# A hybrid decoder trunk on one core: the variance of five layer norms summed with the squares as stationary operand, and the output stored in four parts

## The chip, the cores and the metric

The kernel runs on one NeuronCore of a Trainium2 chip. The metric is the device time of one execution in microseconds (us). The engines are TensorE (PE, its weight loads PEld), VectorE (DVE), ScalarE (ACT), GpSimd (POOL) and SyncE (SP), which only issues DMAs here. Each engine works through its own queue in order; they meet at semaphores.

## The reference, cut to what matters

A two-layer trunk on 1024 tokens of 1024 features (f32). It has five layer norms: one on the input, and two in each layer.

```python
def layer_norm(x, g, b):
    mu = xf.mean(-1, keepdims=True)
    var = jnp.square(xf - mu).mean(-1, keepdims=True)
    return ((xf - mu) * lax.rsqrt(var + LN_EPS) * g + b)

x = layer_norm(x, ln_emb_g, ln_emb_b)
for i in range(2):
    mix = hybrid_mixer(x, ...)
    x = layer_norm(ALPHA * x + mix, ln1_g[i], ln1_b[i])
    ffn = square(relu(x @ mlp_w1[i])) @ mlp_w2[i]
    ple = sigmoid(x @ pe_gate[i] + pe_gate_b[i]) * (p[i] @ pe_proj[i])
    x = layer_norm(ALPHA * x + ffn + ple, ln2_g[i], ln2_b[i])
```

## The kernel before

Activations lie with features on partitions: `Y[:, kt, token]` is feature tile `kt` of 8 (`KT`), and the tokens are two halves of 512 (`hs(hf)`). A sum over features is therefore a product on TensorE: `mean_ones` (128x128, all 1/1024) is stationary, a 128x512 tile moves, and every partition of the PSUM bank receives the sum, already spread over partitions. An f32 product is two PE instructions in the trace.

`layer_norm(u)` is a function in each of four engines' programs; u counts the norms 0 to 4. They share two-buffered tiles `SQ` and run as follows:

- PE: the mean of each half (L621 for u=0, L624 else) into banks 4 and 5. Then, for each half and each `kt`, `mean_ones` times the squares (L629), accumulated in bank 6 + hf.
- DVE: 16 subtractions of the mean (L1613); then for each half, wait for the deviation `STD`, take its reciprocal over 128x512 (L1620), and multiply the eight tiles by it (L1624, or L1628). In norms 1 and 3 the multiplication (L1628), gain and offset (L1631) and the low part `XL` (L1636) of each tile are interleaved on DVE. `XL` of tile kt waits for its high part `XH`, which ACT copies (L1141).
- ACT: squares of half 0 (L1131), square root of each half's bank (L1134), then 16 writes: `XH` in norms 1 and 3, or gain and offset into `X` (L1144) in norms 0, 2 and 4. Norm 0 computes sine tables between root and writes (L1151).
- POOL: the squares of half 1 (L1433).

With the tile counter as semaphore value, square kt waits until the product of square kt - 2 is done.

What follows each norm: norm 0 and norm 2 are followed by the input projection (L669), which takes `X` tile by tile; norm 2 also by the jump back of the layer loop. Norms 1 and 3 are followed on PE by blocks (mt, hf) in the order (0,0), (1,0), (0,1), (1,1), (2,0) and so on: two products with `PE_IN` (L1107, into bank 4 + b; they wait for both square roots while mt < 2), and 24 products of `dense` (L1087 to L1089: high x high, high x low, low x high of each of 8 tiles, fp32r, which is one PE instruction each). Norm 4 is followed by one store of `X`, 4 MB, from SP's queue (L609).

Of the kernel before, what the change touches and what calls it, by code (L numbers as in the profile page):

```python
# [22 lines left out]
ALU = mybir.AluOpType  # L23
ACT = mybir.ActivationFunctionType
# [181 lines left out]
def trunk(nc, xT, pT, pos, w_in, w_uq, w_lr, w_pool, w_out, w_gate, w_pe, w_1, w_2, par, emb, con1, con2, out):  # L206
    cs_dram = nc.dram_tensor("cs_scratch", (2, P, S), F32, kind="Internal").ap()
    with ExitStack() as ctx:
# [3 lines left out]
        def sem(name):  # L212
            return ctx.enter_context(nc.semaphore(name))
# [148 lines left out]
        def met_value(L, n):  # L362
# [3 lines left out]

        ln_sq_later, ln_sum = sem("ln_sq_later"), sem("ln_sum")
        LN_SUMS = 2 + 2 * FB
        ln_mu, ln_xc, ln_sq, ln_sqf, ln_var, ln_std, ln_xn, ln_out = (
            sem(n) for n in ("ln_mu", "ln_xc", "ln_sq", "ln_sqf", "ln_var", "ln_std", "ln_xn", "ln_out"))  # L370

# [170 lines left out]
        @block.sync  # L542
        def _(e):
            e.dma_start(C1[:, :], con1).then_inc(con_landed, 16)
            e.dma_start(EMB[:, :], emb).then_inc(con_landed, 16)
            e.dma_start(BZ[:, 0, :].bitcast(I32), pos.broadcast_to([P, S])).then_inc(pos_landed, 16)
            for hf in range(2):
                e.dma_start(Y[:, :, hs(hf)], xT[:, :, hs(hf)]).then_inc(x_landed[hf], 16)

            def weight_block(L, i):  # L550

                e.wait_ge(w_used, L * W_LAYER + (i + 1))
                settle(e)
                if i < ZW:
                    src = w_in[ds(L, 1), IN_BLOCK[i]]
                elif i < ZW + N_WOUT:
                    src = w_out[ds(L, 1), i - ZW]
                else:
                    src = w_gate[ds(L, 1), i - ZW - N_WOUT]
                e.dma_start(WR[:, i % RING, :, :], src[0]).then_inc(w_landed[i % RING], 16)  # L560

            with e.Fori(0, DEPTH) as L:
                for i in range(RING):
                    weight_block(L, i)

                e.wait_ge(met, met_value(L, -1))
                e.wait_ge(cs_stored, 32)
                e.dma_start(CT[:, :], cs_dram[0]).then_inc(tables_landed, 16)
                e.dma_start(ST[:, :], cs_dram[1]).then_inc(tables_landed, 16)
                e.dma_start(UQ[:, 3:7, :, :], w_uq[ds(L, 1), :, 6:10][0]).then_inc(uqi_landed, 16)  # L570
                e.dma_start(UQ[:, 0:3, :, :], w_uq[ds(L, 1), :, 0:3][0]).then_inc(uq_landed, 16)
                e.dma_start(PAR[:, :], par[ds(L, 1)][0]).then_inc(par_landed, 16)

                for hf in range(2):
                    e.wait_ge(kik_done, L * 2 + (hf + 1))
                    e.dma_start(A3[HD:P, 2, hs(hf)], A3[0:HD, 2, hs(hf)]).then_inc(dup_landed, 16)
                    e.dma_start(IK2[0:HD, hs(hf)], IK2[HD:P, hs(hf)]).then_inc(dup_landed, 16)
                    if hf == 0:
                        weight_block(L, 4)
                        weight_block(L, 5)  # L580
                for i in range(6, ZW + RING - 1):
                    weight_block(L, i)
                e.wait_ge(turned.full, turned.written(L, LAST_Q))
                e.dma_start(LWA[:, :, :, :], w_lr[ds(L, 1)][0, :, 0:2]).then_inc(lora_landed, 16)
                e.dma_start(PW[:, :, :], w_pool[ds(L, 1)][0]).then_inc(lora_landed, 16)
                e.dma_start(LG[:, :, :], w_lr[ds(L, 1)][0, :, 2]).then_inc(lora_landed, 16)
                weight_block(L, ZW + RING - 1)
                e.wait_ge(met, met_value(L, 0))
                for c in range(2):
                    blocks = con2[chunk(c), 0:(6 + LEVELS) * P].rearrange("p (k w) -> p k w", w=P)  # L590
                    e.dma_start(C2P[chunk(c), 0:6 + LEVELS, :], blocks[:, :, chunk(c)]).then_inc(rwkv_landed, 16)
                e.dma_start(i64, con2[:, NC2 - CH:NC2]).then_inc(rwkv_landed, 16)
                e.wait_ge(met, met_value(L, 2))
                settle(e)
                for i in range(ZW + RING, MLP0 - GAP):
                    weight_block(L, i)
                    if i == ZW + N_WOUT + 1:
                        e.wait_ge(d_full[3], L * D_USES + N_WOUT // 2)
                        settle(e)
                        e.dma_start(PE_IN[:, :, :], pT[ds(L, 1)][0]).then_inc(pe_landed, 16)  # L600
                        e.dma_start(PEW[:, :, :, :], w_pe[ds(L, 1)][0]).then_inc(pe_landed, 16)
                with e.Fori(0, FB) as f:
                    for i in range(N_F):
                        e.wait_ge(w_used, L * W_LAYER + f * N_F + (MLP0 + i + 1))
                        src = w_1 if i < FT else w_2
                        e.dma_start(WR[:, i % RING, :, :], src[ds(L * FB + f, 1), i % FT][0])\
                         .then_inc(w_landed[i % RING], 16)
            e.wait_ge(ln_out, 16 * (1 + 2 * DEPTH))
            e.dma_start(out, X[:, :, :]).then_inc(out_stored, 16)  # L609
            e.wait_ge(out_stored, 16)  # L610


        @block.tensor
        def _(e):
            def layer_norm(u, landed=None, sums=None, total=None):

                for hf in range(2):
                    if landed:
                        e.wait_ge(landed[hf], 16)
                        for kt in range(KT):  # L620
                            mm = e.matmul(BK_[4 + hf], mean_ones, Y[:, kt, hs(hf)], start=kt == 0, stop=kt == KT - 1)  # L621
                    else:
                        e.wait_ge(ln_sum, sums + (hf + 1))
                        mm = e.matmul(BK_[4 + hf], mean_ones, total[:, hf, :], start=True, stop=True)  # L624
                    mm.then_inc(ln_mu, 1)
                for hf in range(2):
                    for kt in range(KT):
                        e.wait_ge((ln_sq, ln_sq_later)[hf], u * KT + (kt + 1))
                        e.matmul(BK_[6 + hf], mean_ones, SQ[:, 2 * hf + kt % 2, :], start=kt == 0, stop=kt == KT - 1)\  # L629
                         .then_inc(ln_sqf, 1)  # L630

            e.sem_inc(w_used, RING)
            for b in zbank + wide + [third, narrow, turned] + prep + rb:
# [347 lines left out]
            with e.Fori(0, DEPTH) as L:  # L981
# [119 lines left out]
                for mt, hf in [(0, 0), (1, 0), (0, 1), (1, 1)] + [(mt, hf) for mt in range(2, KT) for hf in range(2)]:  # L1101
                    b = 2 * (mt % 2) + hf
                    if mt < 2:
                        e.wait_ge(ln_std, (L * 2 + 2) * 2)
                    e.wait_ge(pe_free[b], L * 4 + (mt // 2 + 1))
                    for kt in range(2):
                        mm = e.matmul(BK_[4 + b], PEW[:, mt, kt, :], PE_IN[:, kt, hs(hf)], start=kt == 0, stop=kt == 1)  # L1107
# [16 lines left out]
        def _(e):  # L1124
            def layer_norm(u, gain=None, offset=None, dst=None, high=None, between=None):

                for kt in range(KT):
# [1 line left out]
                    if kt >= 2:  # L1129
                        e.wait_ge(ln_sqf, u * 16 + (kt - 1))  # L1130
                    e.activation(SQ[:, kt % 2, :], Y[:, kt, hs(0)], ACT.Square).then_inc(ln_sq, 1)  # L1131
                for hf in range(2):
                    e.wait_ge(ln_sqf, u * 16 + KT * (hf + 1))
                    e.activation(STD[:, hf, :], BK_[6 + hf], ACT.Sqrt, bias=LN_EPS).then_inc(ln_std, 1)  # L1134
                if between:
                    between()
                for n in range(2 * KT):
                    hf, kt = n // KT, n % KT
                    if high is not None:
                        e.wait_ge(ln_out, u * 16 + (n + 1))  # L1140
                        e.activation(high[:, kt, hs(hf)], Y[:, kt, hs(hf)], ACT.Copy).then_inc(high_x, 1)  # L1141
                    else:
                        e.wait_ge(ln_xn, u * 16 + (n + 1))
                        e.activation(dst[:, kt, hs(hf)], Y[:, kt, hs(hf)], ACT.Identity, bias=offset(kt),  # L1144
                                     scale=gain(kt)).then_inc(ln_out, 1)

            def tables():

# [274 lines left out]
        def _(e):  # L1423
            def layer_norm(u):

                for kt in range(KT):
                    e.wait_ge(ln_xc, u * 16 + (KT + kt + 1))
                    if kt >= 2:
                        e.wait_ge(ln_sqf, u * 16 + (KT + kt - 1))
# [176 lines left out]
        def _(e):  # L1606
            def layer_norm(u, between=None, affine=None, high_before=0):
# [6 lines left out]
                         .then_inc(ln_xc, 1)  # L1614
                if between:
                    between()
                for hf in range(2):
                    q = hs(hf)
                    e.wait_ge(ln_std, u * 2 + (hf + 1))
                    e.reciprocal(RST[:, hf, :], STD[:, hf, :])  # L1620
                    e.drain()
                    if not affine:
                        for kt in range(KT):
                            e.tensor_tensor(Y[:, kt, q], Y[:, kt, q], RST[:, hf, :], ALU.mult).then_inc(ln_xn, 1)  # L1624
                    else:
                        for n in range(KT + 3):
                            if n < KT:
                                e.tensor_tensor(Y[:, n, q], Y[:, n, q], RST[:, hf, :], ALU.mult).then_inc(ln_xn, 1)  # L1628
                            if 1 <= n <= KT:
                                gain, offset = affine(n - 1)  # L1630
                                e.tensor_scalar(Y[:, n - 1, q], Y[:, n - 1, q], gain, offset, ALU.mult, ALU.add)\  # L1631
# [504 lines left out]
```

## Time and profile before

| | us |
|---|---|
| median of 3 runs | 3576.71 |
| lowest and highest | 3575.73, 3585.78 |
| the profiled execution | 3576.34 |
| its span | 3574.3 |
| mean granted TensorE clock | 0.965 of full |

A profile is one execution. The chart of waits and the chain of work name, for each idle time, the instruction whose semaphore ended it. The granted clock of a stretch is 1.00 when TensorE is given 2.4 GHz and 0.50 at 1.2 GHz; a value between is a mean over the stretch.

### The profile page before, as it was taken

The numbers are of one execution on the slowest core, as the hardware profiler recorded it, in microseconds if no ns is written. First come the engines' busy times: TensorE is split into PE (matmuls) and PEld (weight loads), VectorE is DVE, ScalarE is ACT, GpSimd is POOL, SyncE is SP. The second block draws the span as 40 slices with busy tenths as digits, with TensorE's granted clock in tenths as the row PEclk, the third lists the DMA queues.
The fourth block names the chain that finished last, engine by engine and source line by source line (L and its number), as shares of the span: only waits on it lengthen the run. The fifth ranks groups of instructions, "written<-read, shape, count | busy, mean of one in ns | idle before, by whom it ended". The sixth has DMA issues, their size and how long they took to land.

```text
span 3574.3 us, 61403 instructions
## 1 busy us (share of the span) xinstructions
PE 3274.0 (92%) x23080; PEld 2373.5 (66%) x23080; DVE 1913.2 (54%) x3061; ACT 1053.9 (29%) x1857; POOL 1146.4 (32%) x952
## 2 busy tenths in 40 slices
PE   7989967999999999999989998689899999999997
PEld 3444435876577888888735444368675788888884
DVE  5788996444623333333467899854526133333335
ACT  3333334442212211211235343344402111221212
POOL 1175632641212222222114755155222122222221
PEclk9999979999999999999999899799999999999998
DMA  3110000001111111111111001000011111111111
GB/s 123 45 33 21 29 23 6 0 1 36 48 36 48 47 47 47 53 47 48 40 55 33 28 24 33 11 6 0 7 31 58 42 51 49 47 47 47 48 46 47
DMA packets 43861, 132.72 MB, mean 37 GB/s; under 512 B 9280, under 2 KB 11840, under 8 KB 43072
## 3 DMA queue, kind: packets, MB, share of 16 engines
q1 hardware_dynamic: 37280, 122.41, 10.5%
q10 hardware_dynamic: 6432, 8.40, 0.9%
q8 instruction: 84, 1.38, 0.2%
q14 instruction: 65, 0.53, 0.0%
HBM read 117.15 MB, written 5.24 MB: 34 GB/s over the span
## 4 chain that ended last, share of the span: by engine, by line
PE 59%; DVE 14%; issue 10%; DVEq 10%; POOLq 2%; ACT 1%; POOL 1%; DMA 1%; PEldq 0%; ACTq 0%; SPq 0%; PEld 0%
DVE M L1715 8%; DVEq L1719 8%; PE wide L1087 7%; PE bank L1089 7%; PE bank L1087 7%; PE bank L1088 7%; PE wide L1089 7%; PE wide L1088 7%; PE wide L799 3%; DVE PB L1735 2%; PE wide L629 2%; PE bank L799 2%; POOLq L1591 1%; DVE WK L1717 1%; DVEq L1716 1%
## 5 line engine op out<-in xcount | busy, mean ns | idle before, releaser
L1590 POOL TENSOR_TENSOR WL<-WR,WH 128x1024 fp32r<-128x1024 f32 x160 | 403.1, 2519 | 1479.2 <-ACT WH L1385 1478.5
L669 PE MATMUL wide<-X,WR 128*128 128x512 f32 (+1 forms) x1088 | 504.7, 608 | 11.6 <-ACT X L1144 9.4
L1385 ACT ACTIVATE WH<-WR 128x1024 fp32r<-128x1024 f32 x160 | 168.2, 1053 | 735.6 <-PE bank L1089 430.2
L2019 DVE TENSOR_TENSOR RB<-RB 128x512 f32<-128x512 f32 x128 | 88.5, 692 | 549.0 <-ACT RB L1411 549.0
L669 PEld LDWEIGHTS wide<-X,WR 128*128 128x128 f32 x1088 | 202.7, 196 | 246.9 <-issue 220.9
L1715 DVE MAX8 M<-WK 128x8 f32<-128x512 f32 (+5 forms) x342 | 314.9, 921 | 23.7
L1717 DVE MATCH_REPLACE8 WK<-M,WK 128x512 f32<-128x512 f32 (+5 forms) x342 | 309.5, 905 | 1.2 <-issue 1.2
L1087 PE MATMUL wide<-XH,WH 128*128 128x512 f32 x640 | 261.6, 409 | 18.1 <-POOLq L1591 9.5
L1087 PE MATMUL bank<-XH,WH 128*128 128x512 f32 x640 | 255.7, 400 | 0.0
L1089 PE MATMUL wide<-XH,WL 128*128 128x512 f32 x640 | 252.8, 395 | 0.0
L1088 PE MATMUL wide<-XL,WH 128*128 128x512 f32 x640 | 252.5, 395 | 0.0
L1089 PE MATMUL bank<-XH,WL 128*128 128x512 f32 x640 | 249.2, 389 | 0.0
L1088 PE MATMUL bank<-XL,WH 128*128 128x512 f32 x640 | 249.0, 389 | 0.0
L1087 PE MATMUL wide<-HH,WH 128*128 128x512 f32 x512 | 201.3, 393 | 0.0
L1088 PE MATMUL wide<-HL,WH 128*128 128x512 f32 x512 | 199.4, 389 | 0.0
L1089 PE MATMUL wide<-HH,WL 128*128 128x512 f32 x512 | 199.4, 389 | 0.0
L1089 PE MATMUL bank<-HH,WL 128*128 128x512 f32 x512 | 199.2, 389 | 0.0
L1088 PE MATMUL bank<-HL,WH 128*128 128x512 f32 x512 | 199.2, 389 | 0.0
L1087 PE MATMUL bank<-HH,WH 128*128 128x512 f32 x512 | 199.2, 389 | 0.0
L2032 DVE TENSOR_TENSOR Y<-Y,bank 128x512 f32<-128x512 f32 x128 | 87.9, 687 | 171.1 <-PE bank L1089 171.1
L799 PE MATMUL wide<-SH 64*64 64x64 f32 x3840 | 153.2, 220 | 21.2 <-POOL SH L1525 14.6
L2032 DVE TENSOR_TENSOR Y<-Y,wide 128x512 f32<-128x512 f32 x128 | 88.0, 687 | 153.7 <-PE wide L1089 153.7
(318 smaller groups left out, 6399.2 us busy)
## 6 DMA issues: line engine op xcount, KB each, us to landing
WR<-in_w SPq DMA_DIRECT2D x128, 512.0 KB, 3.5
WR<-in_w_in SPq DMA_DIRECT2D x34, 512.0 KB, 3.5
WR<-in_w_out SPq DMA_DIRECT2D x16, 512.0 KB, 3.5
WR<-in_w_gate SPq DMA_DIRECT2D x16, 512.0 KB, 5.5
Y<-in_xT SPq DMA_DIRECT2D x2, 2048.0 KB, 13.3
out_T<-X SPq DMA_DIRECT2D x1, 4096.0 KB, 11.1
QZS<-QZ ACTq DMA_DIRECT2D x48, 64.0 KB, 2.0
QZS<-QZ ACTq DMA_DIRECT2D x64, 48.0 KB, 1.9
```

Of the source, the lines that this page charges most:

```text
L669: mm = e.matmul(BK_[hf][:, 0:q.stop - q.start], WR[:, i % RING, kt, :], X[:, kt, q], start=kt == 0, stop=kt == KT - 1)
L799: mm = e.matmul(BK_[bank][chunk(c), j * CH:(j + 1) * CH], lhs[chunk(c), 2 * j + g, :], rhs[chunk(c), 2 * j + g, :], start=True, stop=True)
L1087: e.matmul(BK_[b], WH[:, s, w, :], high[:, kt, q], start=kt == 0, stop=False)
L1088: e.matmul(BK_[b], WH[:, s, w, :], low[:, kt, q], start=False, stop=False)
L1089: mm = e.matmul(BK_[b], WL[:, s, w, :], high[:, kt, q], start=False, stop=kt == kts - 1)
L1385: e.activation(WH[:, split_seq(i) % 2, :, :], WR[:, i % RING, :, :], ACT.Copy).then_inc(w_high, 1)
L1590: e.tensor_tensor(WL[:, s, :, :], WR[:, i % RING, :, :], WH[:, s, :, :].bitcast(F32), ALU.subtract)
L1715: e.max(M8[:, :], src)
L1717: e.match_replace(work, M8[:, :], src, DROPPED if drop else BIG)
L1719: e.drain()
L2019: e.tensor_tensor(RB[:, b, :], RB[:, b, :], RB[:, b, :], ALU.mult).then_inc(square_ready, 1)
L2032: e.tensor_tensor(Y[:, i, hs(hf)], Y[:, i, hs(hf)], BK_[b], ALU.add).then_inc(d_free[b], 1)
```

## The change

Squares and sums: the squares become the stationary operand, 128 tokens at a time, and two columns of `mean_ones` move. So for each half and `kt` there are four products of 128x2, and the bank holds, for token tile t, its sum in column 2t (tokens on partitions). Square root and reciprocal are then taken of 128x8 rather than 128x512. `spread_inverse` brings the inverse back to all partitions: four products of 128x128 with the inverse, broadcast, as stationary and the identity as moving operand, into the same bank. DVE multiplies by that bank.

Order: PE runs `spread_inverse` of half 0 behind tile 1 of half 1, and that of half 1 behind its last tile. ACT takes the squares of the odd tiles of half 1, POOL keeps the even ones. DVE takes the inverse of half 1 behind the multiplication of tile 5 of half 0. In norms 2 and 4, ACT writes three tiles of `X` before the square root of half 1. The store waits for a quarter of `X` four times and stores each by itself.

```diff
+            for n in range(KT // 2, 2 * KT + 1, KT // 2):
+                k, q = slice(...), hs((n - 1) // KT)
+                e.wait_ge(ln_out, 16 * 2 * DEPTH + n)
+                e.dma_start(out[:, k, q], X[:, k, q]).then_inc(out_stored, 16)
# tensor
-                        e.matmul(BK_[6 + hf], mean_ones, SQ[:, 2 * hf + kt % 2, :], start=kt == 0, stop=kt == KT - 1)
+                        for t in range(LN_TOK):
+                            mm = e.matmul(BK_[6 + hf][:, 2 * t:2 * t + 2], SQ[:, 2 * hf + kt % 2, t * P:(t + 1) * P],
+                                          mean_ones[:, 0:2], ...)
+                        mm.then_inc(ln_sqf, 1)
+                        if (hf, kt) in ((1, 1), (1, KT - 1)):
+                            spread_inverse(u, int(kt > 1))
+            def spread_inverse(u, hf):
+                e.wait_ge(ln_inv, u * 2 + (hf + 1))
+                for t in range(LN_TOK):
+                    mm = e.matmul(BK_[6 + hf][:, t * P:(t + 1) * P],
+                                  STD[:, hf, 2 * t:2 * t + 1].broadcast_to([P, P]), ident, start=True, stop=True)
+                mm.then_inc(ln_spread, 1)
# the two PE_IN products of mt < 2
-                        e.wait_ge(ln_std, (L * 2 + 2) * 2)
+                        e.wait_ge(ln_xn, (L * 2 + 1) * 16 + (KT * (hf + 1) if mt else 1))
# scalar, after the squares of half 0
+                ahead = 3 if high is None and not between else 0
+                later_square(1)
+                deviation(0)
+                for kt in range(3, KT, 2):
+                    later_square(kt)
+                for n in range(ahead):
+                    write_out(n)
+                deviation(1)
+                if between:
+                    between()
+                for n in range(ahead, 2 * KT):
+                    write_out(n)
# gpsimd
-                for kt in range(KT):
+                for kt in range(0, KT, 2):
# vector
+                def invert(hf):
+                    e.wait_ge(ln_std, u * 2 + (hf + 1))
+                    e.reciprocal(STD[:, hf, 0:2 * LN_TOK], STD[:, hf, 0:2 * LN_TOK]).then_inc(ln_inv, 1)
+                invert(0)
                 for hf in range(2):
-                    e.wait_ge(ln_std, u * 2 + (hf + 1))
-                    e.reciprocal(RST[:, hf, :], STD[:, hf, :])
+                    e.wait_ge(ln_spread, u * 2 + (hf + 1))
-                            e.tensor_tensor(Y[:, kt, q], Y[:, kt, q], RST[:, hf, :], ALU.mult).then_inc(ln_xn, 1)
+                            e.tensor_tensor(Y[:, kt, q], Y[:, kt, q], BK_[6 + hf], ALU.mult).then_inc(ln_xn, 1)
+                            if (hf, kt) == (0, KT - 3):
+                                invert(1)
```

## Rows read from the trace of the kernel before

**Rows 1.** Lines view: instructions, shapes, count; busy us and mean ns; idle before and its releaser.

```profile
L629 PE MATMUL wide<-SQ,C 128*128 128x512 f32 x160 | 81.2, 634 | 9.1 <-POOL SQ L1433 8.4
L1433 POOL TENSOR_TENSOR SQ<-Y 128x512 f32<-128x512 f32 x40 | 47.9, 1221 | 104.6 <-DVE Y L1613 86.6 <-PE wide L629 16.6 <-issue 1.4
L1620 DVE RECIPROCAL RST<-STD 128x512 f32<-128x512 f32 x10 | 33.5, 3348 | 1.0 <-ACT STD L1134 0.4 <-issue 0.2
L1131 ACT ACTIVATE SQ<-Y 128x512 f32<-128x512 f32 x40 | 25.1, 630 | 85.0 <-DVE Y L1613 70.1 <-PE wide L629 14.9
```

**Rows 2.** A stretch of norm 1: length, busy of PE, PEld, DVE, ACT, POOL; clock; DMA.

```profile
964.00:979.00 15.00, 13.55 (x51) 8.90 (x49) 14.00 (x24) 6.53 (x10) 0.00 (x0) 1.00 0.00 1
```

**Rows 3.** Timeline of norm 1: start, length, engine, line, tiles, count, idle and releaser.

```profile
930.73 9.42 PE L629 MATMUL wide<-SQ,C 128*128 128x512 f32 x20
...
942.53 2.36 DVE L1628 TENSOR_TENSOR Y<-Y,RST 128x512 f32<-128x512 f32 x2
...
948.18 0.60 ACT L1134 ACTIVATE STD<-wide 128x512 f32<-128x512 f32 x1 [9.11 <-PE wide L629]
...
979.93 1.88 PE L1107 MATMUL wide<-PE_IN,PEW 128*128 128x512 f32 x4
...
987.13 1.45 PE L1107 MATMUL wide<-PE_IN,PEW 128*128 128x512 f32 x3
```

**Rows 4.** Timeline of PE around products of two columns and of 128.

```profile
63.28 3.73 PE L656 MATMUL wide<-X,WR 128*128 128x128 f32 x32
...
73.38 3.78 PE L679 MATMUL bank<-A,UQ 128*128 128x128 f32 x16 [4.51 <-DMA UQ<-in_w_uq]
...
483.67 2.84 PE L969 MATMUL wide<-C,SH 128*128 128x2 f32 x24
...
802.25 6.72 PE L969 MATMUL wide<-C,SH 128*128 128x2 f32 x48
```

**Rows 5.** Stretches within those of 802 us, columns as Rows 2.

```profile
805.00:806.00 1.00, 1.00 (x11) 1.00 (x11) 1.00 (x1) 0.19 (x1) 0.01 (x1) 1.00 0.00 0
807.00:808.00 1.00, 1.00 (x7) 1.00 (x6) 1.00 (x2) 0.00 (x0) 0.00 (x0) 0.50 0.00 0
812.00:813.00 1.00, 1.00 (x2) 0.34 (x1) 0.38 (x1) 0.00 (x0) 0.00 (x0) 0.53 0.00 0
```

**Rows 6.** Line view of L969 from 2557.1 to 2559.4: min/median/max ns, first and last start.

```profile
L969 PE MATMUL wide<-C,SH x13: 251/353/353, 2556.9 to 2559.3; 128*128 128x2 f32 x13
```

**Rows 7.** Line view of a small reciprocal.

```profile
L1982 DVE RECIPROCAL G<-G x2: 441/442/443, 815.2 to 2566.0; 128x48 f32<-128x48 f32 x2
```

**Rows 8.** Timeline of norm 0 and what follows it.

```profile
44.08 3.35 DVE L1620 RECIPROCAL RST<-STD 128x512 f32<-128x512 f32 x1 [0.16 <-issue]
...
49.43 1.28 ACT L1151 ACT_TABLE_LOAD   x1
...
53.23 11.39 ACT L1144 ACTIVATE X<-Y,EMB 128x512 f32<-128x512 f32 x16 [0.41 <-ACT BZ L1151]
```

**Rows 9.** Timeline behind norm 2, where the layer loop jumps back.

```profile
1803.98 9.92 PE L669 MATMUL wide<-X,WR 128*128 128x512 f32 x16 [4.07 <-ACT X L1144]
...
1816.30 1.28 ACT L1257 ACT_TABLE_LOAD   x1 [4.48 <-issue]
1817.60 0.60 ACT L1257 ACTIVATE PB<-wide 128x512 f32<-128x512 f32 x1
```

**Rows 10.** Line view: the loop's branch on PE's queue.

```profile
L981 PEldq COMPARE_BRANCH  x2: 67/1760/3454, 1800.2 to 3551.2; - x2
```

**Rows 11.** Timeline of norm 4 and the store.

```profile
3533.23 9.42 PE L629 MATMUL wide<-SQ,C 128*128 128x512 f32 x20
...
3551.44 11.38 ACT L1144 ACTIVATE X<-Y,PAR 128x512 f32<-128x512 f32 x16
```

**Rows 12.** The page's DMA issues: tiles, count, KB each, us to landing.

```profile
WR<-in_w SPq DMA_DIRECT2D x128, 512.0 KB, 3.5
out_T<-X SPq DMA_DIRECT2D x1, 4096.0 KB, 11.1
```

More of the change, by code:

```diff
@@ L368, in trunk @@
         LN_SUMS = 2 + 2 * FB
+        ln_inv, ln_spread = sem("ln_inv"), sem("ln_spread")
+        LN_TOK = HALF // P
+        SQ_ACT = [kt % 2 for kt in range(KT)]
         ln_mu, ln_xc, ln_sq, ln_sqf, ln_var, ln_std, ln_xn, ln_out = (
@@ L607, in _ @@
                          .then_inc(w_landed[i % RING], 16)
-            e.wait_ge(ln_out, 16 * (1 + 2 * DEPTH))
-            e.dma_start(out, X[:, :, :]).then_inc(out_stored, 16)
-            e.wait_ge(out_stored, 16)
+            for n in range(KT // 2, 2 * KT + 1, KT // 2):
+                k, q = slice((n - 1) % KT // (KT // 2) * (KT // 2), (n - 1) % KT + 1), hs((n - 1) // KT)
+                e.wait_ge(ln_out, 16 * 2 * DEPTH + n)
+                e.dma_start(out[:, k, q], X[:, k, q]).then_inc(out_stored, 16)
+            e.wait_ge(out_stored, 4 * 16)
         @block.tensor
@@ L627, in layer_norm @@
                     for kt in range(KT):
-                        e.wait_ge((ln_sq, ln_sq_later)[hf], u * KT + (kt + 1))
-                        e.matmul(BK_[6 + hf], mean_ones, SQ[:, 2 * hf + kt % 2, :], start=kt == 0, stop=kt == KT - 1)\
-                         .then_inc(ln_sqf, 1)
+                        if hf == 0:
+                            e.wait_ge(ln_sq, u * (KT + KT // 2) + (kt + 1))
+                        elif SQ_ACT[kt]:
+                            e.wait_ge(ln_sq, u * (KT + KT // 2) + (KT + kt // 2 + 1))
+                        else:
+                            e.wait_ge(ln_sq_later, u * (KT // 2) + (kt // 2 + 1))
+                        for t in range(LN_TOK):
+                            mm = e.matmul(BK_[6 + hf][:, 2 * t:2 * t + 2], SQ[:, 2 * hf + kt % 2, t * P:(t + 1) * P],
+                                          mean_ones[:, 0:2], start=kt + t == 0, stop=kt + t == KT + LN_TOK - 2)
+                        mm.then_inc(ln_sqf, 1)
[7 more added lines that the diff above has]
+                mm.then_inc(ln_spread, 1)
             e.sem_inc(w_used, RING)
@@ L1131, in layer_norm, with later_square, deviation, write_out @@
                     e.activation(SQ[:, kt % 2, :], Y[:, kt, hs(0)], ACT.Square).then_inc(ln_sq, 1)
-                for hf in range(2):
+                def later_square(kt):
+                    e.wait_ge(ln_xc, u * 16 + (KT + kt + 1))
+                    if kt >= 2:
+                        e.wait_ge(ln_sqf, u * 16 + (KT + kt - 1))
+                    e.activation(SQ[:, 2 + kt % 2, :], Y[:, kt, hs(1)], ACT.Square).then_inc(ln_sq, 1)
+                def deviation(hf):
                     e.wait_ge(ln_sqf, u * 16 + KT * (hf + 1))
[L1134 to L1137, printed above, removed]
+                    e.activation(STD[:, hf, 0:2 * LN_TOK], BK_[6 + hf][:, 0:2 * LN_TOK], ACT.Sqrt, bias=LN_EPS)\
+                     .then_inc(ln_std, 1)
+                def write_out(n):
                     hf, kt = n // KT, n % KT
@@ L1616, in layer_norm @@
                     between()
+                def invert(hf):
+                    e.wait_ge(ln_std, u * 2 + (hf + 1))
+                    e.reciprocal(STD[:, hf, 0:2 * LN_TOK], STD[:, hf, 0:2 * LN_TOK]).then_inc(ln_inv, 1)
+                invert(0)
                 for hf in range(2):
                     q = hs(hf)
-                    e.wait_ge(ln_std, u * 2 + (hf + 1))
-                    e.reciprocal(RST[:, hf, :], STD[:, hf, :])
-                    e.drain()
+                    e.wait_ge(ln_spread, u * 2 + (hf + 1))
                     if not affine:
                         for kt in range(KT):
-                            e.tensor_tensor(Y[:, kt, q], Y[:, kt, q], RST[:, hf, :], ALU.mult).then_inc(ln_xn, 1)
+                            e.tensor_tensor(Y[:, kt, q], Y[:, kt, q], BK_[6 + hf], ALU.mult).then_inc(ln_xn, 1)
+                            if (hf, kt) == (0, KT - 3):
+                                invert(1)
                     else:
@@ L1627, in layer_norm @@
                             if n < KT:
-                                e.tensor_tensor(Y[:, n, q], Y[:, n, q], RST[:, hf, :], ALU.mult).then_inc(ln_xn, 1)
+                                e.tensor_tensor(Y[:, n, q], Y[:, n, q], BK_[6 + hf], ALU.mult).then_inc(ln_xn, 1)
+                            if (hf, n) == (0, KT - 3):
+                                invert(1)
                             if 1 <= n <= KT:
```

## The prediction

> **What bounds the kernel now.** I read the lines view first. The variance products, L629, hold TensorE for 81 us over five norms; half 1's squares come from POOL at 1.04 us each and more, half 0's from ACT at 0.63, and the ten reciprocals of 128x512 cost 3.35 us each, 33.5 in all [rows 1]. The timeline then shows what a norm waits for. In norm 1 the sums start at 930.7, the first multiplication follows at 942.5, the root of half 1 comes at 948.2, 9.1 us after ACT fell idle, and the block (1,1), the first that no longer waits for the norm, starts at 979.9 [rows 3]. Half 1's sums wait for POOL's squares (8.4 of L629's 9.1 idle us) [rows 1]. Behind that DVE is busy for 14.0 of 15 us, for eight tiles of half 1, and sets the end; TensorE is at 2.4 GHz there [rows 2]. So a norm is paced by DVE, POOL and the round trips among them. The change attacks these, and pays on TensorE.
>
> **What a group of sums costs.** Before, one tile costs two instructions, in steady flow one per 0.43 us. Now it is a group of four products, eight instructions of 128x2. The key sums L969 have the same form, also with squares as stationary operand: 24 in 2.84 us, or 0.112 each after the last one's 0.25 [rows 4]. So a group is 0.90 us at full clock, as before. But TensorE doesn't stay at full clock in such products. In the run of 48 from 802.25, PE is busy without a gap, yet the granted clock is 1.00 at 805 and 0.50 at 807, that is 4 us after the first of them; it comes back at 812.9, after some 4 us of products of 512 columns, which start where the 48 end, at 808.9 [rows 4, 5]. The run of 24 ended before that. At 1.2 GHz twelve intervals take 2.4 us, 0.20 to 0.21 each [rows 6], and a group 1.7 us.
>
> Two rules of the Trainium skill bear here. The first is in "TensorE: Matmul & The Clock Gate", section "Back-to-back issue gap": a gap of about 60 cycles for 1 to 64 columns. By that a group would be 8 x 25 ns = 0.2 us; the trace has 0.90, and goes before it. The second is in the same page's "What's actually happening": the engine's clock is throttled by default, and its activity releases it. Taken at its word, an engine without a gap would keep its clock; rows 5 say otherwise. Both are rivals below.
>
> Each norm will have 64 such products in a row, with gaps. I let the clock fall 3 us into them, since they come in looser order than in the key sums. Bounds: at once, and 4 us. Each microsecond later saves 0.9.
>
> **What the rest costs.** `spread_inverse`, eight instructions with 128 columns: 32 of L656 took 3.73 us at full clock, 16 of L679 took 3.78 in a half-clock stretch [rows 4]; so 1.05 us or 1.9 with its tail. The reciprocal of 128x48 takes 0.44 and that of 128x512 3.35; on their line one of 128x8 takes 0.2 [rows 1, 7]. The root of 128x512 takes 0.60 [rows 3]; I give that of 128x8 0.2, the two with their signals 0.5. Below 0.1 or up to 0.8 for both changes a norm by 0.4. Where the changed code multiplies from a PSUM bank, I take no difference.
>
> **Norm 4 at half clock.** Sums start at 3533.2 [rows 11]. In 3 us 3.3 groups pass, 4.7 more take 8.0: half 0 is summed at 3544.4, 11.2 us after the start, where norm 1 before had its first multiplication behind a reciprocal of 3.35 at 11.8. The next two groups, already queued ahead of the spread, take 3.4, the spread 1.9: multiplications from about 3549.4. The remaining six groups take 10.2: half 1 summed at 3559.6. DVE has long done tile 5 and stands at the inverse of half 1; root and inverse 0.5, spread 1.9: 3562.1. ACT has written three tiles ahead and has 13 left from 3559.9 at 11.38/16 = 0.71 [rows 11]: last tile at 3569.3, against 3562.8 (3551.4 + 11.4) before, +6.5. POOL's halved work is not the bound any more.
>
> The store: 4 MB took 11.1 us, 512 KB take 3.5 [rows 12]. On that line 1 MB takes 4.6. The four parts become ready each 2.8 us and move 1 MB at some 2.6 us, so the last one doesn't queue: -6.5 us. Bounds: 3.5 for the quarter, and 11.1 were pieces of 2 KB that bad. Norm 4 in sum: 0, with bounds -1 and +6.
>
> **Norms 1 and 3.** The same to the end of half 1's sums: start 930.7, half 0 at 941.9, spread done 947.2 (before, multiplying began at 942.5), half 1 at 957.4 (before 948.2 [rows 3]). Here two queues hurt. On ACT, `XH` stands behind the root of half 1, as before, so DVE, which needs `XH` of tile 0 behind tile 3, stalls until about 958. And the inverse of half 1 stands on DVE behind tile 5, which is two tiles of 1.9 us (15 us for eight [rows 2]) after the stall: 961.5. PE waits for it, idle, before its second spread: 963.4. Only behind that come the blocks. Before, block (0,0) started at 950 and ran in step with DVE's tiles. Now two `PE_IN` products at half clock (3.4 us), 24 dense products, of which 4 are still slow (0.43) and 20 at 0.23: 973.1. (A block took 7.2 us, 1.7 of it for the four `PE_IN` instructions: 5.5/24 = 0.23 [rows 3].) I give the clock 5 us of this to come back (4 in rows 5). Blocks (1,0) and (0,1) cost 7.2 each; start of (1,1) at 987.5 against 979.9 [rows 3]: +7.6 for each of the two. DVE ends half 1's `XL` at 983 and is covered. Bounds: +5 with the clock falling at 4 us, +9.5 when it falls at once and comes back late.
>
> **Norm 0.** DVE computes the last angle before its inverse until 44.0 [rows 8], and PE waits for it before the first spread. Sums of half 0 and two groups are done by then, so: spread at 45.5 (DVE may be up to 1 us earlier, with fewer POOL squares beside it; I don't count it), six groups 10.2, root, sine tables 3.8 (49.4 to 53.2): first `X` at 60.5, where it was 54.0 (53.2 and its own 0.8) [rows 8]: +6.4. ACT's 16 writes and the projection shift with it. Bounds +5 and +7.5.
>
> **Norm 2.** As norm 4, its second spread ends near 1811.1. Then the loop's branch: it held PE's queue for 3.45 us and the first product came 4.0 after PE's last norm product [rows 9, 10]. So L669 starts at 1815.1, against 1804.0: +11.1. But it then finds `X` complete, and what follows was not PE alone: ACT, behind its last write at 1818.2, takes 4.5 + 1.3 for its own branch and table [rows 9], and copies the projection (`PB`) at about 1824.7, against 1817.6 [rows 9]. So +7.1; bounds +5 and +11.
>
> **Sum**, against the profiled execution: 6.4 + 7.6 + 7.1 + 7.6 + 0 = +28.7. The execution took 3576.3 us (span 3574.3 and 2.0 around it), and 3576.3 + 28.7 = 3605.0. It was within 0.4 us of the median of 3576.7, so I predict **3605**. Other stretches of half clock may move by a few us as everything behind shifts.
>
> **Rivals.**
>
> *The clock holds* (the end on the other side). One mechanism: TensorE stays at 2.4 GHz through the sums. For it: 24 products in 2.84 us; against: the run of 48 from 802 us [rows 4, 5] and a second one, at half clock by 2557 us [rows 6]. Behind it stands the second rule above, of the Trainium skill. Then a norm is faster: half 0's sum in 7.7, half 1 done 16.2 after the start, not 26.4. Norm 4: last write 3559.5, -3.3, and -6.5 of the store: -9.8. Norms 1 and 3: (1,1) at 974.0, -5.9 each. Norm 2: +0.3. Norm 0, tied to the angle: +1.6. Sum -19.7: 3557. It decides from where less than some 4 us of a norm's PE time is slow.
>
> *The clock falls, but late* or rises between the groups, about half of the loss: 3572 to 3588, even at a saving of half the slow groups.
>
> *Narrow products are cheap*, by the skill's gap rule. A group of 0.2 us would be paced by squares at 0.63 to 0.65, half clock or not: sixteen tiles in about 11 us rather than 16: another 4 us for each of norms 1 to 4, 3541. The trace's own 0.112 us per instruction speaks against it.
>
> *The store's small pieces*: a quarter as slow as the whole, +6.5: 3611; it adds to my case and lies in the range.
>
> **How the numbers follow.** My case 0.82, of it 3594 to 3614; the late fall 0.08; the clock holds 0.08; cheap products 0.02. The range is 3589 to 3614: it holds my case with its bounds and part of the late fall, near 0.8. A measurement here can tell 0.3%, 10.7 us. Slower by more: 0.82 and 0.01 of the late fall, 0.83. Within: 0.07. Faster: 0.10.
>
> **What would show it.** In the profile after: granted clock at 0.50 from some 3 us into each norm's products of two columns until about 5 us into the products behind it; mean clock below 0.965. Roots of half 1 near 26 us after the sums start, not 17. In norms 1 and 3 an idle PE of about 4 us before the second spread, ended by DVE's inverse, and DVE waiting for `XH`. L669 behind norm 2 starting 11 us late, `PB` 7. The store's last part landing in 4 to 5 us. I am wrong if the clock is 1.00 through a norm's sums; then all but norm 0 and 2 gain.

## The result, and the profile after

The changed kernel takes 3608.35 us (median, 3606.55 to 3612.89, 4 runs) against 3579.45 us beside it (3575.73 to 3585.78, 4 runs): a ratio of 1.0081, with an interval of 1.0062 to 1.0100. Predicted were 3605 us, between 3589 and 3614, with 0.83 for slower. The profiled execution has a span of 3604.6 us, 30.2 more than before, and a mean granted clock of 0.949 instead of 0.965.

The lines view of the kernel after, with the columns of [rows 1]:

```profile
L640 PE MATMUL wide<-C,SQ 128*128 128x2 f32 x640 | 126.2, 334 | 0.5
L650 PE MATMUL wide<-C,STD 128*128 128x128 f32 x80 | 20.7, 440 | 10.0 <-DVE STD L1661 10.0
L1475 POOL TENSOR_TENSOR SQ<-Y 128x512 f32<-128x512 f32 x20 | 21.1, 1053 | 163.4 <-DVE Y L1655 87.2 <-PE wide L640 76.1
L1685 DVE TENSOR_TENSOR XL<-Y,XH 128x512 fp32r<-128x512 f32 x32 | 22.0, 687 | 13.7 <-ACT XH L1170 13.4
```

L640 holds TensorE for 126.2 us, where L629 held it for 81.2 [rows 1], and hardly ever waits: of the 9.1 idle us before, 8.4 of them ended by POOL's squares, 0.5 are left. The waits went elsewhere. POOL now idles for 76.1 us until TensorE frees a square's buffer (16.6 before), so the producer that seemed to bound the sums waits for them. L650, the spread, waits 10.0 us for DVE's small reciprocal, and L1685 waits 13.4 us for `XH`.

The clock, norm 1 in stretches (columns of [rows 2]):

```profile
938.70:940.40 1.70, 1.64 (x14) 1.64 (x14) 1.70 (x4) 1.09 (x3) 0.97 (x1) 0.92 1.01 424
940.40:954.60 14.20, 14.20 (x68) 14.20 (x68) 6.82 (x13) 3.98 (x8) 2.08 (x2) 0.50 0.53 219
954.60:974.50 19.90, 15.66 (x68) 14.65 (x69) 10.79 (x20) 5.51 (x10) 2.23 (x2) 0.51 0.00 1
974.50:995.00 20.50, 20.50 (x83) 15.21 (x82) 18.52 (x32) 8.30 (x12) 0.00 (x0) 1.00 0.00 0
```

TensorE is busy for all 14.20 us of the second stretch, and the granted clock is 0.50, which is 1.2 GHz. It fell 1.4 us after the first product of two columns (0.92 over the first stretch is a loss in its last 0.3 us) and came back 34.1 us later, 1.5 us into the products of 512 columns. From start to start two successive instructions of the sums are 0.112 us apart where the clock is 1.00, and 0.213 where it is 0.50 (medians of the trace), the half-clock pitch of [rows 6]. Norms 0, 2 and 3 have one such stretch of 34.1 us each, from 2.3, 3.2 and 2.0 us into their sums; norm 4 stays low from 3.8 us into its sums to the end.

The timeline of norm 1, to be laid beside [rows 3]; TensorE first, then ACT, then DVE:

```profile
938.76 15.99 PE L640 MATMUL wide<-C,SQ 128*128 128x2 f32 x80
954.62 2.05 PE L650 MATMUL wide<-C,STD 128*128 128x128 f32 x8
...
970.94 2.08 PE L650 MATMUL wide<-C,STD 128*128 128x128 f32 x8 [4.24 <-DVE STD L1661]
972.81 2.62 PE L1129 MATMUL wide<-PE_IN,PEW 128*128 128x512 f32 x4
...
995.14 1.88 PE L1129 MATMUL wide<-PE_IN,PEW 128*128 128x512 f32 x4
```

```profile
951.38 0.18 ACT L1163 ACTIVATE STD<-wide 128x8 f32<-128x8 f32 x1 [2.20 <-PE wide L640]
...
966.74 0.18 ACT L1163 ACTIVATE STD<-wide 128x8 f32<-128x8 f32 x1 [2.72 <-PE wide L640]
```

```profile
967.46 0.69 DVE L1685 TENSOR_TENSOR XL<-Y,XH 128x512 fp32r<-128x512 f32 x1 [6.36 <-ACT XH L1170]
...
970.69 0.20 DVE L1661 RECIPROCAL STD<-STD 128x8 f32<-128x8 f32 x1
```

Read it backwards from block (1,1), which starts 56.4 us after the sums, 49.2 before. The second spread starts at 970.94 after 4.24 us of idle TensorE, released by the inverse at 970.69. That inverse stands on DVE behind a stall of 6.36 us, ended by ACT's `XH`, which stands behind the root of half 1 at 966.74. That root comes 28.0 us after the sums start, where it was 17.4.

The end, norm 4, beside [rows 11], and the store's row, beside [rows 12]:

```profile
3564.64 14.00 PE L640 MATMUL wide<-C,SQ 128*128 128x2 f32 x80
3578.50 2.06 PE L650 MATMUL wide<-C,STD 128*128 128x128 f32 x8
...
3591.09 2.08 PE L650 MATMUL wide<-C,STD 128*128 128x128 f32 x8 [0.51 <-DVE STD L1661]
```

```profile
out_T<-X SPq DMA_DIRECT2D x4, 1024.0 KB, 4.2
```

### The profile page after: what moved, and what is told of

Its sections match the earlier page's. It is cut to its first block, busy times and chain, and to the rows that moved or that the text cites. A ratio compares the mean times of both kernels' runs of the same rounds, so it can differ in the third digit from the quotient of the medians.

```text
span 3604.6 us, 62540 instructions
## 1 busy us (share of the span) xinstructions
PE 3328.3 (92%) x23640; PEld 2487.9 (69%) x23640; DVE 1870.1 (52%) x3061; ACT 1061.5 (29%) x1877; POOL 1119.3 (31%) x932
## 4 chain that ended last, share of the span: by engine, by line
PE 59%; DVE 15%; issue 10%; DVEq 10%; POOLq 2%; ACT 1%; POOL 1%; DMA 1%; ACTq 1%; PEldq 0%; SPq 0%; PEld 0%
DVE M L1764 8%; DVEq L1768 8%; PE wide L1109 7%; PE bank L1111 7%; PE bank L1110 7%; PE bank L1109 7%; PE wide L1110 7%; PE wide L1111 7%; PE wide L821 3%; PE wide L640 3%; DVE PB L1784 2%; PE bank L821 2%; POOLq L1633 1%; DVE WK L1766 1%; DVEq L1765 1%
```

## The experiments

Each kernel was timed beside the kernel before on its own chip (3576 to 3577 us in every group), with intervals of 0.0009 to 0.0013 on either side of the ratio (0.0032 in run 1). "Block (1,1)" is its start after the start of norm 1's sums: 49.2 before, 56.4 after. Run 2, whose norms 1 and 3 have the code of the kernel before, has 50.3 and 49.9, so such a start is known to about 1 us.

**1. A product of 512 columns behind every group.** The changed kernel and one unused product:

```diff
                         mm.then_inc(ln_sqf, 1)
+                        e.matmul(BK_[0][:, 0:HALF], ident, C1[:, 0:HALF], start=True, stop=True)
```

> The changed kernel with one idle product of 128x512 (f32, ident x 512 constant columns, two instructions, 0.85 us at 2.4 GHz) behind each group of four narrow products; its result is read by nobody. My theory (narrow products let the clock fall, and that is where the time goes): granted clock near 1.00 through every norm's sums; a group and its filler take 0.90 + 0.85 = 1.75 us, as long as the group alone at half clock (1.71), so the roots of half 1 still come some 26 to 28 us after the sums start; but spreads take 1.05 rather than 1.9 and the products behind the norm start at full clock: 3 to 4 us less in norms 1 and 3, 1 to 4 in the others, about 3596 (3590 to 3603), though 80 products were added. Rival (the amount of TensorE work, waits or order cost the time, not the clock): the 80 products add up to 68 us, 3640 to 3676.

Measured: 3646.03 us (3621.67 to 3675.85, 6 runs), 1.0222 [1.0190, 1.0253]. Windows of its profile, two from norm 1 and two from norm 3:

```profile
937.40:952.00 14.60, 14.60 (x86) 10.78 (x86) 8.40 (x15) 4.98 (x9) 1.91 (x2) 1.00 0.63 258
952.00:972.00 20.00, 16.73 (x93) 12.55 (x94) 9.83 (x18) 4.88 (x9) 3.27 (x3) 0.95 0.00 1
2702.40:2716.00 13.60, 13.60 (x47) 9.74 (x47) 8.20 (x14) 3.02 (x5) 1.90 (x2) 0.55 0.67 276
2716.00:2738.00 22.00, 22.00 (x69) 15.80 (x69) 0.89 (x2) 2.59 (x5) 1.04 (x1) 0.50 0.00 1
```

The gain that I expected didn't come, and the median lies in the rival's range. The one profile is of the fastest run (3621.67 us). In four of its five norms the clock held through the sums, but a group with its filler takes 1.75 us at full clock, as long as a bare group at half clock, so root and block (1,1) stay at 28.2 and 56.7. That 16 fillers of 0.85 us move block (1,1) by only 0.3 us against the changed kernel speaks against the rival: the amount of work isn't what costs there. In norm 3 the clock fell all the same, and block (1,1) came at 73.3: one fall costs 16.6 us between two norms of the same code. A different number of norms that fall from run to run would give the spread of the six runs. Their mean clocks fit that (0.966 at 3621.67 us, 0.960 and 0.961 at 3643 to 3647, 0.952 at 3675 and 3676), but it isn't shown. The filler doesn't tell the clock's price, since it adds as much work as it saves.

**2. The store alone.** The kernel before with the output stored in four parts.

```diff
-            e.wait_ge(ln_out, 16 * (1 + 2 * DEPTH))
-            e.dma_start(out, X[:, :, :]).then_inc(out_stored, 16)
+            for n in range(KT // 2, 2 * KT + 1, KT // 2):
+                ...
+                e.dma_start(out[:, k, q], X[:, k, q]).then_inc(out_stored, 16)
```

> The kernel before with only the store in four parts. My theory: the last 1 MB lands 4 to 5 us behind the last tile of X instead of 11.5: -6.8 us, 0.19% faster. Rival (pieces of 2 KB or four issues cost what they save): within 2 us of before.

Measured: 3568.29 us (3565.16 to 3576.87), 0.9980 [0.9971, 0.9989], each part landing 4.2 to 4.3 us after its issue. The store is worth about 7 us, as expected: 7.2 by the ratio (3.2 to 10.4 by its interval), and 6.9 from the last `X` to the end of the span.

**3. Wide sums, all else of the change.** The changed kernel with the old product of 512 columns, root and reciprocal of 128x512 and no spread, so that the `PE_IN` products wait for the roots again; the squares are still shared by ACT and POOL, ACT writes three tiles ahead, and the store is in four.

```diff
-                        for t in range(LN_TOK):
-                            mm = e.matmul(BK_[6 + hf][:, 2 * t:2 * t + 2], SQ[...], mean_ones[:, 0:2], ...)
+                        e.matmul(BK_[6 + hf], mean_ones, SQ[:, 2 * hf + kt % 2, :], ...)
```

> The changed kernel with the old wide sums (mean_ones stationary, 512 columns move), the old root of 128x512 and the old reciprocals of 3.35 us, without spreads; the division of the squares between ACT and POOL, the order on ACT and the store in four parts stay. My theory: clock at 1.00 in the sums; roots of half 1 come 16 to 17 us after the sums start rather than 27. Norm 0 -3, norms 1 and 3 about -1.5 each, norm 2 -1, norm 4 -1 and -6.8: about 14 us below before, 3562 (3556 to 3570). Rival (the order and the division of the squares are what costs): 3585 or more.

Measured: 3566.49 us (3560.45 to 3569.33), 0.9964 [0.9952, 0.9977], block (1,1) at 48.7. Expected were 3562, and 1.5 us for each of norms 1 and 3, where 0.5 came. Its lines:

```profile
L639 PE MATMUL wide<-SQ,C 128*128 128x512 f32 x160 | 76.8, 615 | 8.7 <-POOL SQ L1471 8.2
L1658 DVE RECIPROCAL RST<-STD 128x512 f32<-128x512 f32 x10 | 33.5, 3349 | 2.1 <-ACT STD L1159 1.5 <-issue 0.2
```

All of the loss is gone with the narrow products. POOL's squares still end most of the sums' idle time (8.2 of 8.7 us, before 8.4 of 9.1), though it has only half of them now. Against the store alone the shared squares and the writes ahead are worth 2 us by the medians and 6 by the ratios; the two intervals overlap.

**4. Wide sums, and the inverse turned.** The root of half a norm is turned to tokens on partitions by four products of two columns, inverted as 128x8 and spread; in norms 1 and 3 the second time inside block (0,0), with `XH` three tiles ahead. The root is taken eight times too large, since the turning product adds up 128 equal roots, each times 1/1024, and so returns an eighth of it.

```diff
+            def turn_deviation(u, hf):
+                e.wait_ge(ln_std, u * 2 + (hf + 1))
+                for t in range(LN_TOK):
+                    mm = e.matmul(BK_[6 + hf][:, 2 * t:2 * t + 2], STD[:, hf, t * P:(t + 1) * P], mean_ones[:, 0:2], ...)
+                mm.then_inc(ln_var, 1)
```

> Wide sums at full clock, and only the inverse goes the narrow way: root of 128x512 on ACT, four narrow products turn it to tokens on partitions, reciprocal of 128x8, spread by four products of 128x128. In norms 1 and 3 the second inverse is made inside block (0,0), where TensorE waits for DVE anyway, and ACT writes three tiles of XH ahead of the root of half 1; in norm 0 both inverses come behind all sums. My theory: no 3.35 us reciprocals on DVE and no lost clock: norm 0 -4.5, norms 1 and 3 -6 each, norm 2 0 to +2, norm 4 -9.6: 3551 (3545 to 3560). Rival (the spread's round trips PE-DVE-PE cost what the reciprocals did): near the wide-sum kernel, 3560 to 3570.

Measured: 3568.80 us (3563.41 to 3574.89), 0.9973 [0.9963, 0.9982]. Block (1,1) comes at 45.2, 4 us earlier, so the small reciprocal does pay in norms 1 and 3. Norms 0 and 2 lose it: the projection waits behind the spreads and starts 26.8 us after the sums, where the wide kernel of run 3 had 23.2 and 20.6. Against run 3, the stretches that begin with norms 1 and 3 are 3.8 us shorter each, those of norms 0 and 2 are 5.0 and 3.8 longer, and in norm 4 the last `X` ends 1.4 us later: nothing is left of the gain. Half of what separates the result from my 3551 us is norm 0, which I had at 4.5 us less than before; its stretch is 4.7 longer.

**5. The columns alone.** The changed kernel with 128 moving columns instead of two; ACT reads two of each 128.

```diff
-                            mm = e.matmul(BK_[6 + hf][:, 2 * t:2 * t + 2], SQ[:, 2 * hf + kt % 2, t * P:(t + 1) * P],
-                                          mean_ones[:, 0:2], ...)
+                            mm = e.matmul(BK_[6 + hf][:, t * P:(t + 1) * P], SQ[:, 2 * hf + kt % 2, t * P:(t + 1) * P],
+                                          mean_ones, ...)
```

> The changed kernel with 128 moving columns instead of 2 in each product of the variance sums: the same 64 instructions and four stationary tiles a norm and half, nothing added in front of or behind them, 64 times the columns. Theory: an instruction of this kind costs 0.11 us at full clock because each brings a new stationary tile, so the sums lose nothing by the columns, and the engine, now full of columns, keeps 2.4 GHz. Then the root of half 1 comes 16 to 17 us after a norm's sums start instead of 26 to 28, and the time is about 3560 (3555 to 3568). Rival 1: the loss isn't the clock's but that of the form (squares as stationary operand, two spreads and their waits), and the time stays at 3600 to 3610. Rival 2: 128 columns are not hidden behind the weight load, so that a group costs twice as much with a clock that holds: 3590.

Measured: 3566.46 us (3563.54 to 3568.06, 6 runs), 0.9966 [0.9954, 0.9978]. The line of its sums; then a stretch of norm 0's sums and two of norm 1:

```profile
L640 PE MATMUL wide<-C,SQ 128*128 128x128 f32 x640 | 80.0, 283 | 3.7 <-POOL SQ L1476 3.2
```

```profile
42.00:49.00 7.00, 5.51 (x26) 5.51 (x27) 4.59 (x9) 0.00 (x0) 1.04 (x1) 0.51 0.00 1
935.00:944.50 9.50, 9.50 (x81) 9.27 (x82) 8.36 (x15) 5.03 (x9) 2.52 (x3) 1.00 0.96 395
944.50:952.30 7.80, 6.94 (x58) 6.37 (x56) 4.55 (x7) 1.97 (x5) 2.55 (x3) 1.00 0.01 4
```

and its timeline:

```profile
935.00 9.66 PE L640 MATMUL wide<-C,SQ 128*128 128x128 f32 x80
944.49 1.06 PE L650 MATMUL wide<-C,STD 128*128 128x128 f32 x8
...
956.42 1.70 PE L650 MATMUL wide<-C,STD 128*128 128x128 f32 x8 [4.24 <-DVE STD L1662]
```

This is the run that decides. The number of instructions, the stationary tiles, the waits and their order are those of the changed kernel; with 64 times the columns the granted clock is 1.00, eighty instructions take 9.66 us instead of 15.99, L640 is busy for 80.0 us instead of 126.2, and the kernel is 42 us faster (41 by the ratios). The clock holds through the sums of norms 1 to 4. In norm 0, where TensorE idles before the first spread, it is low for a part of them, and there the instructions of 128 columns are 0.213 us apart, elsewhere 0.112: at either clock the pitch is that of two columns. The root of half 1 comes at 17.2, block (1,1) at 45.7. What costs is the clock; the form, the spreads and their waits alone don't, for the time is that of the wide sums (0.9966 and 0.9964). Why the columns decide on the clock isn't shown; only 2 and 128 were tried. The time is 6 us above my 3560, and inside the range. The 4.24 us of idle before the second spread are still there.

**6. The order alone, and 7. order and columns.** In norms 1 and 3, `XH` is written three tiles ahead of the root of half 1, DVE inverts half 1 behind tile 7, and the second spread stands inside block (0,0).

```diff
-                ahead = 3 if high is None and not between else 0
+                ahead = 0 if between else 3
...
+                def tile_ready(kt, hf):
+                    if hf == 0 and kt == 6:
+                        spread_inverse(L * 2 + 1, 1)
+                    e.wait_ge(low_x, L * 16 + (hf * KT + kt + 1))
```

> The changed kernel with only the order of norms 1 and 3 mended: ACT writes three tiles of XH ahead of the root of half 1, DVE inverts half 1 behind tile 7 instead of tile 5, and TensorE spreads it inside block (0,0), before the product of its tile 6. The sums keep their 2 columns, so the clock should fall as before (34 us of half clock in each of the first four norms). Theory: of the 7.2 us that a norm lost, the two misplaced waits (XH behind the root, 6.4 us of DVE idle; the second spread ahead of all blocks, 4.2 us of PE idle) are worth some 5 to 6, which the slow sums alone don't cost: block (1,1) starts about 51 us after the sums instead of 56.4, and the time is about 3597. Rival: the half clock alone sets the end, the block starts follow the sums whatever the order: 3605 to 3610.

> Both: 128 columns in the sums and the order of norms 1 and 3 mended. Theory: with the clock held, half 1 is summed by 17 us, so the misplaced waits cost little (the inverse behind tile 5 comes at about 25 us anyway), and the order is worth 1 to 3 us a norm beyond the columns alone: 3555. Rival: costs add, and the order brings the same 10 to 12 us here as with the clock low: some 3548.

Measured: order alone 3602.57 us (3598.49 to 3604.14), 1.0066 [1.0054, 1.0078]; with the columns 3561.03 us (3557.96 to 3567.21), 0.9955 [0.9942, 0.9967]. The clock falls in the order's run as it does in the changed kernel:

```profile
944.50:956.00 11.50, 11.50 (x60) 11.50 (x60) 8.16 (x14) 4.75 (x8) 1.86 (x2) 0.55 0.80 328
956.00:975.00 19.00, 19.00 (x81) 17.46 (x81) 8.74 (x16) 4.95 (x10) 3.27 (x3) 0.50 0.00 0
```

With runs 5 to 7, norm 1 is a table of two by two (block (1,1), us after the sums start):

| | 2 columns | 128 columns |
|---|---|---|
| order of the change | 56.4 | 45.7 |
| order mended | 53.3 | 43.5 |

The columns, and so the clock, are worth 10 to 11 us in norm 1, the order 2 to 3. I had expected 5 to 6 from the order alone (block (1,1) at 51, 3597 us), and neither came. Two rows of DVE in that run say why:

```profile
962.45 1.47 DVE L1680 TENSOR_TENSOR Y<-Y,wide 128x512 f32<-128x512 f32 x2 [4.92 <-PE wide L650]
...
970.31 0.69 DVE L1690 TENSOR_TENSOR XL<-Y,XH 128x512 fp32r<-128x512 f32 x1 [3.46 <-ACT XH L1175]
```

and one of ACT:

```profile
969.13 0.63 ACT L1164 ACTIVATE SQ<-Y 128x512 f32<-128x512 f32 x1 [2.78 <-PE wide L640]
```

The stall for `XH` has shrunk from 6.36 to 3.46 us and isn't gone: ahead of the root, `XH` still stands behind ACT's share of half 1's squares, the last at 969.13, and those wait for the slow sums to free their buffer. DVE, which multiplies from 18.0 us after the sums start, needs two halves of some 15 us and this stall, ends `XL` at 52.5 and so sets block (1,1). The wait for the spread is hidden inside block (0,0). For run 7 I had expected 3555 and got 3561. The order's part came (5.4 us against run 5, for 5); it was run 5 that stood 6 us above its forecast. The norm 3 of run 7 has block (1,1) at 44.8, not 43.5: there the clock is 0.50 from 25.1 to 28.5 us after the sums start, and the second spread takes 1.81 us instead of 1.05.

**8. Wide sums, the turned inverse in norms 1 and 3 only,** as in run 4; norms 0, 2 and 4 as in run 3.

> The old wide sums in all norms, squares split between ACT and POOL and the output in four parts as in the changed kernel. In norms 1 and 3 alone the root is turned by four narrow products, inverted as 128x8 and spread by products, the second time inside block (0,0); norms 0, 2 and 4 keep root and reciprocal of 128x512. Theory: the two parts of the earlier runs add. Wide sums everywhere gave 3566.5; the turned inverse moved block (1,1) of norms 1 and 3 from 48.7 to 45.2 us after the sums' start, 3.5 us each, so 3559.5. Rival: the earlier kernel with the turned inverse had the same gain in norms 1 and 3 and was no faster in the end, because what follows (clock, weights' ring) takes it back: 3566.

Measured: 3558.17 us (3551.92 to 3560.29), 0.9939 [0.9926, 0.9951], block (1,1) at 45.1. The parts add as expected (3559.5), and the rival, that what follows takes the gain back, is out: what took it back in run 4 was norms 0 and 2.

**9. The fastest found.** Run 7, with the wide sums in norm 0, and root and reciprocal of 128x512 and no spread there.

```diff
+                        if landed:
+                            e.matmul(BK_[6 + hf], mean_ones, SQ[:, 2 * hf + kt % 2, :], ...).then_inc(ln_sqf, 1)
+                            continue
                         for t in range(LN_TOK):
```

> The kernel of the last but one run (128 columns in the sums, norms 1 and 3 in the mended order), but norm 0 with the old wide sums, the root and reciprocal of 128x512 and no spread. In norm 0 of that kernel the first inverse waits behind the sine angle on DVE (43.2), and the columns were no help: the root of half 1 came 22.9 us after the sums' start and the projection's copy 39.9, where the wide sums had 17.9 and 35.3. Theory: norm 0 is worth those 4.6 us, the rest stays: 3556. Rival: the projection of norm 0 isn't what the following work waits for, and nothing is gained: 3561.

Measured: 3553.54 us (3549.20 to 3556.38, 5 runs), 0.9938 [0.9924, 0.9951]: 23 us faster than the kernel before. Block (1,1) is at 43.5 in norms 1 and 3 alike. From norm 0's sums to norm 1's it takes 4.9 us less than run 7, where I expected 4.6. The ratio is that of run 8 within 0.0001, so these two, timed on different chips, aren't told apart.

## Why the prediction was right

**The clock.** The step that decided was that TensorE, though never idle, loses its clock in products of two columns [rows 4, 5]. The profile after shows it in all five norms, and run 5 shows that it is the cause: the same instructions with more columns keep 2.4 GHz. I let it fall after 3 us; it fell after 1.4 (norm 1) to 3.8 (norm 4), inside my bounds. I let it return 5 us into the dense products; it was 1.5 in norm 1, 2.7 in norm 3 and 4.5 in norms 0 and 2. By the Trainium skill ("TensorE: Matmul & The Clock Gate", section "What's actually happening") activity releases the throttle; the trace agrees where products of 512 columns follow, and differs in the sums of two columns, where TensorE is busy for 14.20 of 14.20 us and the clock is 0.50.

**A group's cost.** I had 0.90 us at full and 1.7 at half clock; the pitch of 0.112 and 0.213 us makes it 0.90 and 1.71. The same page of the Trainium skill states a gap of some 60 cycles, 25 ns, for 1 to 64 columns (section "Back-to-back issue gap"). It isn't seen here. The page gives it for a product by itself, without the load of a stationary tile, and each of these products brings one, so as a rival for this form it was weak from the start.

**The sum by its terms.** The span grew by 30.2 us. Cut at the starts of the five norms' sums, that is:

| | predicted | measured |
|---|---|---|
| ahead of norm 0 | 0 | +0.7 |
| norm 0 to norm 1 | +6.4 | +7.3 |
| norm 1 to norm 2 | +7.6 | +6.9 |
| norm 2 to norm 3 | +7.1 | +9.7 |
| norm 3 to norm 4 | +7.6 | +6.8 |
| norm 4 to the end | 0 | -1.2 |

In norms 1 and 3, block (1,1) came 7.2 and 7.3 us later, through the chain that was written down, but two misses in it cancel. The sums of half 1 ended later than I had them (the root at 28.0, after sums that I let end at 26.7), and the second spread started at 32.2 instead of 31 or so; block (0,0) then took 7.9 us instead of 9.7, for the clock came back sooner. DVE's last `XL`, which I called covered at 52.3, ended at 55.0 and was just covered. I took no difference for multiplying from the PSUM bank; a multiplication takes 0.69 us there, where it took 0.79 from `RST`. With `RST` and the shared squares (run 3) it takes 0.75 in norms 1 and 3, so the bank is a part of that and not all. In norm 4 the last `X` came +5.7 us for +6.5, and the store gave -6.9 for -6.5.

**Norm 2: right by luck.** The projection's copy came +7.1 us later, as predicted, and its first product +11.2 for +11.1. But my own terms for the copy, 1818.2 + 4.5 + 1.3, make 1824.0 and not 1824.7, so +6.4. What filled the gap is that ACT took 6.8 us from its last write to the copy, not 5.8: its idle time before the table load is 5.5 us, where it was 4.5. Why wasn't followed. The sum should have been 28.0. (The steps for norm 4, too, end 0.3 us earlier than the same steps for norm 1.) And from norm 2's sums to norm 3's it takes 9.7 us longer, of which the copy explains 7.1.

**How firm single stretches are.** The stretches between the norms vary too. From norm 2's sums to norm 3's, runs 5 and 7 have the same code, but take 903.4 and 894.3 us, at mean clocks of 0.94 and 0.95; the kernel before and run 2 differ by 3.0 us there. So a time of one profile is known to 5 us or so outside the norms, the 2.6 us that are left over behind norm 2 can't be told from that, and my sum hit the time closer than it had a right to.

**The rival "the clock holds".** Run 5 is this rival made real. I priced it at 3557; it takes 3566. Its norm 4 came as worked out (9.7 us less than before, store included, for 9.8), but norms 1 and 3 gained 3.5 each, not 5.9. There the term was mis-sized: I put block (1,1) at 43.3 after the sums, and run 5 has 45.7. The inverse of half 1 behind DVE's tile 5 keeps the second spread until 956.42, 4.2 us after the root, whatever the clock. Run 7, where it is out of the way, has 43.5. By the start of norm 1's sums it has lost 4.3 us, where I had +1.6, and from norm 2's sums to norm 3's 4.0, where I had +0.3. In spans: I had -19.7, and it is -9.1 (3565.2 - 3574.3); of the 10.6 between, norms 1 and 3 are 4.1, norm 0 2.7 and the stretch behind norm 2 3.7, which is within what that stretch varies. The other rivals are excluded: the late or broken fall by one unbroken stretch of 34.1 us in each of the first four norms, from 1.4 to 3.2 us on; cheap narrow products by the pitch of 0.112 us at full clock; small pieces in the store by its 4.2 us.

## What to carry to other kernels

A busy engine isn't a fast one. Before an operation is turned so that the moving side becomes tiny, look in the trace for a run of the same form that lasts longer than a few microseconds and read the granted clock in it; if it falls, the other engines' gains are paid back on TensorE, here 10 us in norm 1. Where each instruction brings a stationary tile of its own, more moving columns can cost nothing: from 2 to 128 the pitch stayed at 0.112 us, the clock held, and the kernel gained 42 us. And when several engines hand work around in a norm, a small step such as the inverse should stand where its consumer first needs it and nothing stalls ahead of it; but mending one wait is worth only what the next one in the chain lets through.

## What the hardware showed that I had not expected

128 f32 columns behind a fresh stationary tile of 128x128 cost as little as two: 0.112 us from start to start at full clock in run 5 and in the changed kernel, and 0.213 at half clock in both. One fall of the clock can cost 16.6 us (run 1: 56.7 and 73.3 for the same code), and a filler of 512 columns behind each group held the clock in four norms of five in the one profile, not in all. A store of 1 MB lands in 4.2 us, in less than half of the whole's 11.1.
